# Windowed attention of the two last layers in pairs of heads, with score matmuls on separate halves of the array and the sink as a key column

## What is computed

```python
s_loc = jnp.einsum('bnqhgd,bnkhd->bnhgqk', qb, kw).astype(jnp.float32) * SCALE_A
s_loc = jnp.where(mask[None, :, None, None], s_loc, NEG_INF)       # |key - query| <= 128
s_ctx = jnp.einsum('bnqhgd,blhd->bnhgql', qb, k_ctx).astype(jnp.float32) * SCALE_A
p = jax.nn.softmax(jnp.concatenate([s_loc, s_ctx, s_sink], axis=-1), axis=-1)
o = (jnp.einsum('bnhgqk,bnkhd->bnqhgd', p_loc, vw) + jnp.einsum('bnhgql,blhd->bnqhgd', p_ctx, v_ctx))
```

## Time and profile before

| | |
|---|---|
| time, median of 3 runs | 2798.91 us (2795.23 to 2802.09) |
| profiled execution: time, span | 2794.96 us, 2792.9 us |
| TensorE (PE) busy | 2558.9 us, 92% of the span |
| VectorE (DVE), ScalarE (ACT), GpSimd (POOL) busy | 41%, 32%, 18% |
| windowed attention, layer 0 | 1434.8 to 1541.4 us |
| windowed attention, layer 1 | 2387.3 to 2473.7 us |

### The profile page before, as it was taken

The page is one execution under the profiler, slowest core; times in us unless marked ns, Lnnn a source line. Parts: engine busy times, 40 slices in busy tenths (PEclk is TensorE's granted clock), DMA queues, the critical chain, the costliest instruction groups (busy, mean ns, idle before and its releaser), DMA issues.

```text
span 2792.9 us, 33849 instructions
## 1 busy us (share of the span) xinstructions
PE 2558.9 (92%) x13806; PEld 1987.9 (71%) x13806; DVE 1149.4 (41%) x1929; ACT 898.4 (32%) x1617; POOL 515.6 (18%) x393
## 2 busy tenths in 40 slices
PE   6887888979999988999999999999788999999998
PEld 5755656757788775568876888888565577678876
DVE  4647553433333244542156313323345433643433
ACT  3326442332332223442136211113224432442222
POOL 2004122130110211230013110013312210221023
PEclk8998898989999989999999999999889999999998
DMA  4221143234522310101200122123110123013222
GB/s 155 77 92 35 42 136 104 74 125 151 166 91 91 115 27 23 38 16 53 83 23 1 52 67 71 46 62 112 62 27 23 38 61 106 8 39 117 79 91 90
DMA packets 188619, 200.57 MB, mean 72 GB/s; under 512 B 15632, under 2 KB 183272, under 8 KB 187954
## 3 DMA queue, kind: packets, MB, share of 16 engines
q1 hardware_dynamic: 185426, 180.32, 20.7%
q10 hardware_dynamic: 3040, 18.09, 1.6%
HBM read 187.91 MB, written 10.49 MB: 71 GB/s over the span
## 4 chain that ended last, share of the span: by engine, by line
PE 82%; DVE 7%; ACT 5%; issue 3%; POOL 2%; DMA 1%; ACTq 0%; SPq 0%; POOLq 0%; DVEq 0%
PE PS L628 20%; PE PS L629 20%; PE PS L631 20%; PE PS L696 6%; PE PS L723 4%; PE PS L709 3%; PE PS L980 2%; DVE ST L1587 1%; ACT SA L1136 1%; PE PS L670 1%; POOL RB L2142 1%; DVE RB L1538 1%; PE PS L768 1%; POOL XTc L2272 1%; PE PS L1000 1%
## 5 line engine op out<-in xcount | busy, mean ns | idle before, releaser
L628 PE MATMUL PS<-HH,WH 128*128 128x512 f32 x2144 | 795.5, 371 | 35.3 <-POOL HL L2147 22.7
L629 PE MATMUL PS<-HL,WH 128*128 128x512 f32 x2144 | 762.7, 368 | 0.0
L631 PE MATMUL PS<-HH,WL 128*128 128x512 f32 x2144 | 693.8, 367 | 0.0
L1528 DVE TENSOR_TENSOR WL<-WB,WH 128x2048 fp32r<-128x2048 f32 (+2 forms) x150 | 312.1, 2081 | 640.7 <-ACT WH L1069 640.0
L628 PEld LDWEIGHTS PS<-HH,WH 128*128 128x128 f32 x2144 | 404.7, 189 | 153.0 <-issue 31.8
L629 PEld LDWEIGHTS PS<-HL,WH 128*128 128x128 f32 x2144 | 405.3, 189 | 75.8 <-issue 1.9
L631 PEld LDWEIGHTS PS<-HH,WL 128*128 128x128 f32 x2144 | 366.6, 189 | 46.3
L1069 ACT ACTIVATE WH<-WB 128x2048 fp32r<-128x2048 f32 (+2 forms) x150 | 256.2, 1708 | 362.5 <-PE PS L631 279.4
L2167 POOL TENSOR_SCALAR SA<-SA,ST 128x768 f32<-128x768 f32 (+3 forms) x80 | 141.1, 1764 | 452.9 <-DVE ST L1601 452.9
L2142 POOL TENSOR_TENSOR RB<-RB,SA 128x512 f32<-128x512 f32 (+2 forms) x68 | 87.8, 1291 | 447.1 <-ACT SA L1086 444.9
L1587 DVE TENSOR_REDUCE ST<-PS 128x1 f32<-128x768 f32 (+5 forms) x192 | 111.8, 583 | 131.9 <-PE PS L696 84.2
(11 more groups left out here) (309 smaller groups left out, 3391.4 us busy)
## 6 DMA issues: line engine op xcount, KB each, us to landing
WB<-in_w_in_dram SPq DMA_DIRECT2D x67, 1024.0 KB, 5.3
WB<-in_w_ff_dram SPq DMA_DIRECT2D x32, 1024.0 KB, 5.4
WB<-in_w_mod_dram SPq DMA_DIRECT2D x24, 1024.0 KB, 7.5
WB<-in_w_branch_dram SPq DMA_DIRECT2D x24, 512.0 KB, 3.4
WB<-in_w_o_dram SPq DMA_DIRECT2D x8, 1024.0 KB, 5.2
XTc<-xd ACTq DMA_DIRECT2D x2, 3072.0 KB, 10.2
WB<-in_cmp_w_dram SPq DMA_DIRECT2D x4, 1024.0 KB, 5.6
WB<-in_w_mkv_dram SPq DMA_DIRECT2D x4, 1024.0 KB, 5.3
```

What stands on the lines that cost most here:

```text
L628: pe.matmul(D[0:m, o:o + w], h, xh[:, o:o + w], start=k == 0, stop=False)
L629: pe.matmul(D[0:m, o:o + w], h, xl[:, o:o + w], start=False, stop=False)
L631: t = pe.matmul(D[0:m, o:o + w], lo, xh[:, o:o + w], start=False, stop=k == b.kt - 1)
L1528: dve.tensor_tensor(WL[s % NH][:, 0:b.kt, 0:b.cols], WB[b.n % NW][:, 0:b.kt, 0:b.cols], WH[s % NH][:, 0:b.kt, 0:b.cols].bitcast(F32), ALU. ...
```

## The change

The attention of branch a gets a function of its own on each engine, `attend_pairs`, and a class `Pairs`.

- KA holds each key head twice, in the lower and the upper 64 partitions, and no zeros. The scores of a head are a matmul over 64 partitions, and those of the two heads of a pair are issued in turn, one on the lower and one on the upper half of the array's rows. The memset of KA on GpSimd goes.
- The sink is a key column in front of the near keys: a matmul over one partition (ones times the sink) writes one column. The exponential, the minimum and the addition for the sink go. The reduction, the exponential and the multiply are over 513, 641 or 257 columns.
- A pair's masks come behind all its scores, and one signal tells that both heads' scores are there.
- A step is a pair. The scores of pair s use PS0 and PS1 and wait for the exponential of the odd head of pair s-1. The transposes are of pair s-2, the outputs of pair s-3.
- The copies of transposed groups are shared out by unit and group: ScalarE takes the even unit's first group and the odd unit's second, VectorE the others. PTa has 4 buffers, and the probabilities have 6 (4 of SA, 2 of SD).
- One reciprocal serves both heads.

```diff
-                QA, KA, VA = sb("QA", 128, 4, NT, scope=sy), sb("KA", 128, 4, NT, scope=sy), sb("VA", 128, 6, 128, scope=sy)
+                QA, KA, VA = sb("QA", 128, 4, NT, scope=sy), sb("KA", 128, 2, NT, scope=sy), sb("VA", 128, 6, 128, scope=sy)
...
-                        q, K = QA[:, p, n * 128:(n + 1) * 128], KA[:, 2 * kvh + h % 2, :]
+                        q, K = QA[64 * e:64 * e + 64, p, n * 128:(n + 1) * 128], KA[64 * e:64 * e + 64, kvh, :]
...
+                        qk.insert(0, (511 - wl, 1, cm("ones")[64 * e:64 * e + 1, :], SK[64 * e:64 * e + 1, 0, h:h + 1]))
...
+            def by_vector(self, u, g):
+                return (u + g) % 2 == 1
...
+            def attend_pairs(A):                                   # TensorE
...
+                for s in range(A.steps + 3):
+                    if s < A.steps:
+                        us = (2 * s, 2 * s + 1)
+                        if s:
+                            pe.wait_ge(*at("ex", A.name, 2 * s - 1))
...
+                        for c in range(len(A.units[us[0]]["qk"])):
+                            for u in us:
+                                o, n, q, k = A.units[u]["qk"][c]
+                                t = pe.matmul(A.S(u)[:, o:o + n], q, k, start=True, stop=True)
+                        for u in us:
+                            for o, n, mask in A.units[u]["masks"]:
+                                t = pe.matmul(A.S(u)[:, o:o + n], cb("b_ident"), mask, start=False, stop=True, skip_group_check=True)
+                        t.then_inc(*done("qk", A.name, s))
+                    if 0 <= s - 2 < A.steps:
+                        for u in (2 * s - 4, 2 * s - 3):
+                            parts, src = A.units[u]["parts"], A.pb(u)
+                            pe.wait_ge(*at(*A.scaled(u)))
+                            for g in range(0, len(parts), 4):
+                                before = A.turn[u, g // 4] - 2
+                                if before >= 0:
+                                    pe.wait_ge(*at(*A.turned(*A.groups[before])))
...
+            def attend_pairs(A, after_put, ready):                 # ScalarE
...
+                for s in range(A.steps + 3):
+                    if s < A.steps:
+                        for u in (2 * s, 2 * s + 1):
...
+                            act.activation(Pb[:, lo:w], A.S(u)[:, lo:w], ACT.Exp, bias=A.stat(u, 0), accum_out=A.stat(u, 1)).then_inc(*done("ex", A.name, u))
+                    if 0 <= s - 2 < A.steps:
+                        for u in (2 * s - 4, 2 * s - 3):
...
+                                if not A.by_vector(u, g // 4):
...
+                                    act.activation(A.PT[u % 4][0:w, c:e], A.T(u, g // 4)[0:w, 0:e - c], ACT.Copy).then_inc(*done("pt_a", A.name, u, g // 4))
...
+            def attend_pairs(A):                                   # VectorE
...
+                    if s < A.steps:
+                        dve.wait_ge(*at("qk", A.name, s))
+                        for u in (2 * s, 2 * s + 1):
+                            lo, hi = A.units[u]["span"]
+                            dve.tensor_reduce(A.stat(u, 0), A.S(u)[:, lo:hi], AX.X, ALU.max, negate=True).then_inc(*done("mx", A.name, u))
...
-                pool.wait_ge(*at("lin", f"b1{l}", 7))
-                pool.memset(KA[:, :, :], 0.0).then_inc(*done("kzA", l))
-                pool.wait_ge(*at("kzA", l))
+                pool.wait_ge(*at("yl", 1, l, 3))
```

More of the change, by code:

```diff
@@ L447, in build, with unit @@
         nts = (NT, NX)
-        def unit(qk, span, parts, m, put, ready=(), sink=None, gate=None, first=True, last=True, rowmask=False):
-            return dict(qk=qk, span=span, parts=parts, m=m, put=put, ready=list(ready), sink=sink,
-                        gate=gate, first=first, last=last, rowmask=rowmask)
+        def unit(qk, span, parts, m, put, ready=(), gate=None, first=True, last=True, rowmask=False):
+            return dict(qk=qk, span=span, parts=parts, m=m, put=put, ready=list(ready), gate=gate,
+                        first=first, last=last, rowmask=rowmask)
         def fresh(units):
@@ L580, in stat, with __post_init__, S, T @@
                 return (ST[:, i, c:c + 1] for c in range(4))
+        @dataclass
+        class Pairs:
+            name: str
+            units: list
+            PT: list
+            PB: Any
+            base: int
+            def __post_init__(self):
+                self.n, self.groups, self.turn, self.outs, o = len(self.units), [], {}, [], -1
+                for u, un in enumerate(self.units):
+                    for g in range(0, len(un["parts"]), 4):
+                        self.turn[u, g // 4] = len(self.groups)
+                        self.groups.append((u, g // 4))
+                    if u % 2 == 0:
+                        o += un["first"]
+                        self.outs.append(o)
+                self.steps = self.n // 2
+            def S(self, u):
+                return PS[u % 2]
+            def T(self, u, g):
+                t = self.turn[u, g] % 2
+                return PS[2][:, 512 * t:512 * t + 512]
+            def O(self, p):
+                o = self.outs[p] % 2
+                return PS[3][:, 512 * o:512 * o + 512]
+            def by_vector(self, u, g):
+                return (u + g) % 2 == 1
+            def turned(self, u, g):
+                return ("pt_d" if self.by_vector(u, g) else "pt_a", self.name, u, g)
+            def last_turn(self, u):
+                return ("tp", self.name, u, (len(self.units[u]["parts"]) - 1) // 4)
+            def scaled(self, u):
+                return ("sc_p" if u % 2 else "sc_d", self.name, u)
+            def put(self, p):
+                return ("put", self.name, *self.units[2 * p]["put"])
+            def pb(self, u):
+                return self.PB[u % 6]
+            def last_in(self, i):
+                return self.last_turn(max(u for u in range(self.n) if u % 6 == i))
+            def stat(self, u, c, n=1):
+                i = (self.base + u) % 64
+                return ST[:, i:i + n, c]
         kinds = [("nsa", nsa_units(), True, 2, PTn, PBn), ("mem", mem_units(), True, 1, PTm, PBm)]
@@ L584, in build @@
             kinds += [(f"b{l}{half}", b_units(l, half), False, 2, PTb, None) for half in range(2)]
[L585 removed]
+            kinds += [(f"a{l}", a_units(l), False, 0, PTa, SA + SD[0:2])]
         att, base = {}, 0
         for name, units, narrow, pair, PT, PB in kinds:
[L588 removed]
+            att[name] = Attention(name, units, narrow, pair, PT, PB, base) if pair else Pairs(name, units, PT, PB, base)
             base += len(units)
@@ L2179, in attend, with attend_pairs @@
                 drain(fill)
+            def attend_pairs(A):
+                for u in range(1, A.n, 2):
+                    un = A.units[u]
+                    lo, hi = un["span"]
+                    Pb = A.pb(u)[:, lo:hi]
+                    pool.wait_ge(*at("rr", A.name, u // 2))
+                    pool.tensor_scalar(Pb, Pb, A.stat(u, 3), None, ALU.mult).then_inc(*done("sc_p", A.name, u))
             pool.memset(ST[:, :, :], 0.0).then_inc(*done("set0"))
```

121 lines of the change are left out of this document (90 added, 31 removed).

## The result

The changed kernel takes 2835.96 us (median of 4 runs, 2834.36 to 2838.44) against 2799.42 of before (4 runs, 2795.23 to 2802.09): a ratio of 1.0133, with a 95% interval of 1.0115 to 1.015. It is slower by 37 us. The profiled execution took 2834.47 us, with a span of 2832.7.

A forecast was written before the change was run, and what follows sets the result against it. It took the stages to be close to TensorE's own list of work. To 2794.96 us it added 15 (longer steps and drain) and 12 (lowered clock), 2822, then 3.95 for the median: 2826 us, range 2794 to 2852.

The forecast's parts named there:

- The loop of a pair: Scores, then both heads' softmax before the next pair's scores: 4.67 us (n = 1, 2), 4.01 (n = 0, 3), 2.65 (n = 4, 5).
- Rival (d): Both stages: TensorE's list remains the bound, the softmax of a pair stays hidden; faster, 2785 us, chance 0.10.
- nearly every pair: Sign in both stages: TensorE waits for ScalarE's exponential at nearly every pair.
- the wait for the copy passes 2 us: Sign: TensorE waits for the PTa copy over 2 us at every pair after n = 1 and 2.
- The stall: Odd head's transposes wait for ScalarE's copy: n = 3 takes 6.29 us, n = 4 5.14, n = 0 of layer 1 6.50.
- the forecast's 1 us for the end of layer 1: Last two pairs of layer 1 drain with the copy wait and no cover: some +1 us.
- The row halves: Score matmuls: both halves of the array's rows overlap fully, 0.44 us (256 keys) or 0.65 (384) for both heads.
- rival (c): Score passes and key columns: row halves do not overlap, +59 us, 2858 us, chance 0.10.
- The key column: Opening of each pair: two loads and a change of shape, so scores begin at 0.43 us; priced at 0.42 a pair.
- Rival (b): Opening of each pair: key column and its changes of shape are free; 2797 us, no change, chance 0.12.
- The clock: TensorE's granted clock in both stages falls to 0.89, and its 100 us on the path grow by 12.
- rival (a): Both stages: TensorE's clock holds; only +15 us, 2814 us, chance 0.23.

The follow-up runs named there:

- The first experiment: Changed kernel with separate transpose banks for even and odd head, fifth blocks in the free output bank: 2790.62 us, 0.9973 of before.
- the third experiment: Changed kernel with both heads' scores read from rows 0 to 63, the odd head's scores left out: 2904.26 us.
- the run with the hidden fillers: Changed kernel with unread identity transposes in TensorE's idle places, except ahead of outputs in steps waiting for ScalarE's copy: 2818.92 us.

## Why the prediction was right

The forecast was slower, 2826 us in a range of 2794 to 2852; it is 2836.

**The loop of a pair** held to 0.02 us: 4.66 and 3.99 where 4.67 and 4.01 were worked out, with TensorE waiting for the odd head's exponential. That closeness is partly luck: the key column was 0.12 us too dear (below), but VectorE starts at 2.03 and 1.70 where 2.06 and 1.75 were forecast, since the passes and masks behind it took some 0.1 longer than their rows. Rival (d), that TensorE's list stays the bound, does not hold. The first experiment met one of its conditions, the stall absent, and came out at 2790.6, near its 2785, but not by its mechanism: TensorE still waits 0.86, 1.64 and 1.21 us for an exponential at three of six steps.

Among the signs, "nearly every pair" was too much: TensorE waited for an exponential at half of the pairs, three of six in a cycle, which are the three steps that the forecast's own sum had put at the loop. And the wait for the copy passes 2 us at n = 3 (2.35), not at n = 4 (1.52).

**The stall** was placed and sized rightly: 6.26 and 5.14 against 6.29 and 5.14. For n = 0 of layer 1 no step at the full clock exists in the changed kernel; the run with the hidden fillers read 6.41 against 6.50. A cycle of layer 0 is 2.1 us longer than before and one of layer 1 about 1.2. With four of each, and the forecast's 1 us for the end of layer 1, which ran partly at the low clock and gives no reading of it, the structure costs 14 to 15 us, as summed. Taking the wait away gave back 45 us, because the shortened steps go below those of before and the clock rises with them.

**The row halves** overlap fully, by the third experiment, and rival (c) is out.

**The key column** was put at 0.42 us and measured 0.31 to 0.32 by the steps. The scores start 0.31 after the first load, not 0.43. With the key column over 64 rows they start at 0.25, so leaving the 1-row shape takes 0.06 where the sum had 0.10, and the three loads take 0.25 where it had 0.33; how that divides among the loads, the runs don't tell. Rival (b), that it is free, is out.

**The clock** is the term of the sum that was mis-sized. It was taken as 0.89, from one stretch with the same busy share, and put at 12 us. The busy share came out as expected, 76 and 74%, but the granted clock was 0.83 and 0.87, so rival (a), that the clock holds, is out. What is left of the 38 us after 15 of structure is 23, and the fillers alone recovered 17 of them while 31 of 70 us at the low clock stayed. The windows of the changed kernel, each stage cut in its start and its steady part, show where the low clock lies.

```profile
1435.80:1469.30 33.50, 24.72 (x138) 17.41 (x138) 12.36 (x25) 9.81 (x27) 8.16 (x4) 0.54 0.00 1
1469.30:1564.40 95.10, 73.48 (x698) 54.73 (x696) 45.30 (x105) 41.03 (x124) 33.37 (x20) 0.93 0.00 1
2410.20:2440.00 29.80, 19.11 (x122) 12.89 (x124) 12.46 (x25) 9.82 (x26) 8.15 (x4) 0.75 0.00 1
2440.00:2512.80 72.80, 56.47 (x554) 43.40 (x550) 32.99 (x66) 28.78 (x78) 24.68 (x12) 0.91 0.00 1
```

In the steady parts the clock is 0.93 and 0.91, a little above the forecast's 0.89. At the starts it is 0.54 and 0.75: 31 and 15 us at 1.2 GHz, 46 of the 70. There the pipeline fills, TensorE waits for the rope, for the first exponentials and for the first stalls, and the prediction had not looked at it. What the starts cost can be read from the key columns: of n = 0 in the first and second cycle of layer 0, and of n = 1 in the first and second cycle of layer 1.

```profile
1435.92 0.38 PE L827 MATMUL PS<-SK,CM 1*128 1x1 f32 x4 [1.60 <-DVE SD L1714]
...
1472.20 0.38 PE L827 MATMUL PS<-SK,CM 1*128 1x1 f32 x4
...
2414.59 0.59 PE L827 MATMUL PS<-SK,CM 1*128 1x1 f32 x4 [2.35 <-ACT SA L1286]
...
2442.03 0.43 PE L827 MATMUL PS<-SK,CM 1*128 1x1 f32 x4
```

These cycles take 36.3 and 27.4 us, where a cycle at the full clock takes 27.9 and 22.0: 8.3 and 5.4 too long, 14 of the 23. At 0.89 the forecast's 14.5 and 10.4 us of TensorE on the path grow by 3. The steady parts cost the other 9, about what the forecast had for them. So the term that was too small is "at 0.89 that grows by 12", one clock for a whole stage, steady part and start alike; 23 in place of 12 is the 10 us by which the forecast missed. That 0.89 came near in the steady parts is partly luck, since a busy share does not give the clock (last section).

## What to carry to other kernels

When two units of work are joined into one step, list what each engine has queued ahead of the copy that frees a buffer: the gain of the joined matmuls was lost because a copy went behind two exponentials and the buffers were too few for both. Here the buffers were changed; moving the copy ahead of the exponentials was not tried. Give the joined units banks of their own before judging the joining, and try the same banks on the old form: here it came to the same time without the pairs. And count the idle time that a new wait brings to TensorE twice, once as itself and once in the granted clock, also at the start of a stage.

## What the runs showed of the hardware

The busy share of TensorE does not tell its clock. With both heads on one half of the rows it was busy 142 of 167 us (85%) in layer 0 and had a clock of 0.69. With pairs and own banks it was busy 82% at 0.93, and the kernel before with those banks 93% at 1.00. Busy time in the records grows when the clock is low (the same key column reads 0.59 us and 0.38), which is part of it, but not all: the added work there, passes over half of the array, came with a lower clock instead of a higher one. Which property of these passes does it was not tried.

One microsecond at 1.2 GHz costs less than the half that a TensorE-bound stretch would lose: 17 us for 40 with the fillers (0.4), and 34 us for 95 with one row half (0.36). In the changed kernel's steps n = 1 to 4 of layer 0's first cycle, all at the low clock, it is less: 28.8 us against 20.7 at the full clock, 8.1 for 28.8 (0.28). Softmax goes on at its own speed: an exponential of 641 columns takes 0.79 us in those steps, as in the others, while the eight score passes before it take 2.51 instead of 1.35.
